# Loading the next expert's bound during the current expert's products, in the expert loop of a hybrid encoder layer

## What is computed

```
g = einsum('td,edf->tef', h, w_gate)      # w_gate: 64 x 1024 x 256
u = einsum('td,edf->tef', h, w_up)        # w_up:   64 x 1024 x 256
a = silu(g) * u * comb[..., None]         # comb is 0 but for a row's 6 experts
routed = einsum('tef,efd->td', a, w_down) # w_down: 64 x 256 x 1024
return routed + shared
```

## Time and profile before

| | us |
|---|---|
| median of 3 runs | 1249.72 |
| lowest and highest run | 1246.98, 1256.64 |
| the profiled execution, its own time | 1252.91 |
| its span, from the first instruction to the last | 1251.1 |
| TensorE busy in the span | 1103.7 |
| expert loop, first to last item's start (line 956) | 553.68 to 1152.70 |

### The profile page before, as it was taken

The page is one execution under the profiler, slowest core; times in us unless marked ns, Lnnn a source line. Parts: engine busy times, 40 slices in busy tenths (PEclk is TensorE's granted clock), DMA queues, the critical chain, the costliest instruction groups (busy, mean ns, idle before and its releaser), DMA issues.

```text
span 1251.1 us, 19602 instructions
## 1 busy us (share of the span) xinstructions
PE 1103.7 (88%) x6547; PEld 688.2 (55%) x6548; DVE 385.2 (31%) x932; ACT 338.1 (27%) x762; POOL 306.6 (25%) x500
## 2 busy tenths in 40 slices
PE   4899999898999997479999889999999989999960
PEld 1675675465675643355655455555555545555730
DVE  3100000383543224532222222222222212222687
ACT  3100100495664102212222222322323222322111
POOL 1000100102232000053333323333333323333032
PEclk9899999897987899779999999999999999999995
DMA  8711311403440003818889999998889999798652
GB/s 347 277 68 67 143 68 68 140 5 135 156 182 1 1 1 138 329 49 317 317 335 415 415 410 411 409 391 315 317 343 394 410 413 390 291 415 313 286 171 75
DMA packets 77741, 304.18 MB, mean 243 GB/s; under 512 B 13271, under 2 KB 15385, under 8 KB 59465
## 3 DMA queue, kind: packets, MB, share of 16 engines
q1 hardware_dynamic: 60792, 268.26, 54.8%
q0 software_dynamic: 16256, 33.08, 7.1%
q10 hardware_dynamic: 656, 2.36, 0.5%
HBM read 290.26 MB, written 33.82 MB: 259 GB/s over the span
## 4 chain that ended last, share of the span: by engine, by line
PE 75%; DMA 12%; DVE 7%; issue 2%; ACT 2%; POOL 1%; SPq 1%; POOLq 0%; DVEq 0%; ACTq 0%
PE bank L956 23%; PE bank L963 12%; DMA arena<-in_w_down 8%; PE bank L641 6%; PE bank L642 6%; PE bank L707 4%; PE bank L894 4%; PE bank L949 3%; DMA arena<-in_w_in 2%; PE bank L818 2%; PE bank L968 2%; DVE arena L1695 1%; PE bank L845 1%; PE bank L794 1%; PE bank L607 1%
## 5 line engine op out<-in xcount | busy, mean ns | idle before, releaser
L956 PE MATMUL bank<-arena 128*64 128x256 f32 x2880 | 336.0, 386 | 38.3 <-DMA arena<-in_w_down 17.8
L956 PEld LDWEIGHTS bank<-arena 128*64 128x64 f32 x2880 | 243.8, 139 | 163.1 <-issue 106.7
L963 PE MATMUL bank<-arena 128*64 128x512 f32 x728 | 176.3, 602 | 1.6 <-DVE arena L1652 0.8
L1658 DVE COPY arena<-bank 128x512 f32<-128x512 f32 x90 | 62.3, 692 | 365.2 <-PE bank L949 365.2
L1246 ACT COPY arena<-bank 128x128 f32<-128x128 f32 x90 | 23.9, 265 | 412.3 <-PE bank L968 412.3
L517 POOL DMA_INDIRECT arena<-h_rows,arena x93 | 98.2, 1056 | 82.7 <-POOL arena L514 78.2
L525 POOL DMA_INDIRECT y_rows<-arena x91 | 93.2, 1024 | 86.0 <-POOL arena L522 81.3
L641 PE MATMUL bank<-arena 128*128 128x288 f32 x320 | 105.5, 412 | 3.7 <-DMA arena<-in_w_in 3.7
L642 PE MATMUL bank<-arena 128*128 128x288 f32 x320 | 104.8, 410 | 0.0
L1652 DVE COPY arena<-bank 128x512 f32<-128x512 f32 x91 | 63.0, 692 | 102.1 <-PE bank L963 102.1
L963 PEld LDWEIGHTS bank<-arena 128*64 128x64 f32 x728 | 52.0, 136 | 67.4 <-issue 66.4
(11 more groups left out here) (279 smaller groups left out, 1157.2 us busy)
## 6 DMA issues: line engine op xcount, KB each, us to landing
arena<-in_w_gate SPq DMA_DIRECT2D x64, 1024.0 KB
arena<-in_w_up SPq DMA_DIRECT2D x64, 1024.0 KB
arena<-in_w_down SPq DMA_DIRECT2D x64, 1024.0 KB
arena<-in_w_ada SPq DMA_DIRECT2D x8, 2048.0 KB, 7.8
arena<-in_w_in SPq DMA_DIRECT2D x6, 2048.0 KB, 16.1
arena<-in_w_ada SPq DMA_DIRECT2D x8, 1024.0 KB, 17.3
arena<-y_rows SPq DMA_DIRECT2D x2, 3072.0 KB, 13.2
arena<-in_w_out SPq DMA_DIRECT2D x2, 2048.0 KB, 7.7
```

Of the source, the lines that this page charges most:

```text
L956: last = pe.matmul(bank[0][n * SLOT:n * SLOT + SLOT, 0:2 * P].rearrange("p (g f) -> p g f", f=P), HGT[:, k % 4, k // 4, :], w[:, :, n * P: ...
L963: last = pe.matmul(bank[3][n * SLOT:n * SLOT + SLOT, :], AE[:, f, :], DN[j][:, f, 512 * n:512 * n + 512], start=(f == 0), stop=(f == 1))
L1658: dve.tensor_copy(hgt, bank[1][:, :]).then_inc(hgt_ready, 1)
```

## The change

`item` gets an argument `ahead`. Where it is given, the engine loads `START[ahead]` between the gate and up products and the transpose of `turn_out`, and `item` returns the register. In the expert loop, `lo` and `hi` are loaded once per turn of four experts, ahead of j = 0. The first item of the experts j = 0, 1, 2 loads `START[e + j + 2]`, which is the bound of expert j + 1; after each expert the names move on: what was `hi` is now `lo`, and what was loaded is `hi`. The item of j = 3 and the items of the inner loop load nothing.

```
-            def item(i, j, before):
+            def item(i, j, before, ahead=None):
...
                 gate_up(j)
+                after = pe.value_load(START[0:1, bass.ds(ahead, 1)], min_val=1, max_val=NI) if ahead is not None else None
                 turn_out()
...
                 down(before)
+                return after
...
             with pe.Fori(0, NE // 4) as g:
                 e = g * 4
+                lo = pe.value_load(START[0:1, bass.ds(e, 1)], min_val=0, max_val=NI - 1)
+                hi = pe.value_load(START[0:1, bass.ds(e + 1, 1)], min_val=1, max_val=NI)
                 for j in range(4):
-                    lo = pe.value_load(START[0:1, bass.ds(e + j, 1)], min_val=0, max_val=NI - 1)
-                    hi = pe.value_load(START[0:1, bass.ds(e + (j + 1), 1)], min_val=1, max_val=NI)
                     pe.wait_ge(exp_ld[j], (g + 1) * 48)
                     pe.sem_inc(pe_mark)
-                    item(lo, j, (j + 3) % 4)
+                    after = item(lo, j, (j + 3) % 4, e + (j + 2) if j < 3 else None)
                     with pe.If_lt(pe.to_reg(lo + 1), pe.to_reg(hi)):
                         with pe.Fori(lo + 1, hi) as i:
                             item(i, j, j)
+                    lo, hi = hi, after
```

## The result

The changed kernel took 1245.51 us (median of 20 runs, 1238.94 to 1251.91), the kernel before, in 20 runs beside it, 1254.12 us. The ratio is 0.9937 with a 95% interval of 0.9921 to 0.9952: 7.9 us less, between 6.0 and 9.9. The forecast was 6.4 us less.

The account below looks back on a forecast made before the run. In the expert loop TensorE sets the pace in some stretches, the stream of weights in others. Of 15.5 us of gaps 6.4 are kept, 9.1 lost, the added load costs 0: 1243.3 us against the median 1249.72, range 1236 to 1250.5.

Parts of the forecast that it names:

- Part 1: At the 48 expert starts j = 1, 2, 3 no load is left; start to start becomes 6.10 us unless weights are late.
- The sum of 15.5 us: Total of 40 boundary gaps, the gain's upper bound; 8 of the 48 starts, ended by weights, are left out.
- Part 2: One load, 0.7 us, between gate-and-up and the transpose, 48 times; covered by the sequencer's lead of 2.2 us, cost 0.
- Part 3: Gaps summed by stretch of the expert loop: 6.4 us kept, 9.1 us lost where weights set the pace.
- 4.70 us: The 11 gaps from 643 to 822 us, DMA share 1.01, forecast as lost to longer waits for weights.
- halving the term: In 822 to 980 us, 4.08 us kept less half of the 2.30 behind 926, as DMAs idle little there: 2.93.
- A: Rival: TensorE is the bound throughout and all 40 gaps count; gain 15.5 us, time 1234.2, chance 0.09.
- B: Rival: weights take nearly all, also in 822 to 980 and 1025 to 1077; 2.4 us remain, time 1247.3, chance 0.13.
- C: Rival: longer waits lower TensorE's clock more often, two more places costing 3.4 us; gain 3.0, time 1246.7, chance 0.12.
- the sign that I gave for it: For the rival on the clock: more than two gate-and-up items (line 956) over 5 us.
- D: Rival: the load ahead of the transpose is not covered, 0.7 us each; +7 us, time 1256.7, chance 0.04.
- The 11 us: Issue gaps forecast to be left in the loop, from 17.0 us: those of the tops, 0.8 each.

Follow-up runs that it names:

- light_after: Changed kernel with only an eighth of the up weights loaded from the fifth expert on: 1211.90 us, ratio 0.9676 to the kernel before.
- dose6: Changed kernel with the load behind gate and up made six times instead of once: 1321.31 us, ratio 1.0594 to the kernel before.
- half: Kernel before with lo taken over from the last hi, so one load stays at the boundary, none behind gate and up: 1242.43 us, ratio 0.9929.
- rep: Changed kernel run again unaltered, for a second profile and more times: 1246.01 us, ratio 0.9956 to the kernel before.
- light: Pair with an eighth of the up weights loaded from the fifth expert on: kernel before 1232.60 us, changed kernel 1211.90 us.
- split: Pair with the down weights on a semaphore of their own, waited for ahead of the down products: kernel before 1248.98 us, changed kernel 1234.49 us.
- split_hoist: Changed kernel with a semaphore of their own for the down weights and no bound loads at the tops: 1226.98 us, ratio 0.9784.
- split_before: Kernel before with a semaphore of their own for the down weights, waited for ahead of the down products: 1248.98 us, ratio 0.9967.
- split_early: split_hoist with the wait for the down weights moved ahead of the wait for the evacuated transpose: 1218.89 us, ratio 0.9723 to the kernel before.

## Why the prediction was right, point by point

**Part 1, the loads that go: right.** Starts in time are at 6.10, VectorE's product is late next and leaves no gap. The sum of 15.5 us is near what light_after shows: 18.9 in the loop, where the 8 starts that the sum left out count too. Of these 8, 7 are ended by weights. The eighth (1028.04) is late because the item ahead of it is the slow one at 1019.91; the profile shows 0.20 us of issue there and no wait for weights, so its gap belonged into the sum (some 0.3 to 0.4 us).

**Part 2, the load that comes in costs 0: right.** The lead fell from 2.26 to 1.49 us, where 1.5 was forecast, and dose6 shows what it covers. But the argument missed that the boundary itself has room for one load (half): the cover was not needed. The Trainium skill, "DMA: Bandwidth & Descriptors", section "Latency and other measured facts", has a floor of about 600 ns for a tensor load; the rows have 0.31 us for the instruction, which is under that floor, and 0.65 to 0.77 with its arithmetic, and the measurement decides. As forecast, nothing hung on it.

**Part 3, the split into kept and lost: right in its pattern, three terms off.** I compare the loops by the starts of the same items: of before and after in the profiles shown, and of the second profile (rep). Starts in the kernel before, then in the changed kernel, of the first item of experts 0, 8, 29, 44, 55 and 62 (numbered from 0):

```profile
553.68 6.29 PE L956 MATMUL bank<-arena 128*64 128x256 f32 x32 [1.73 <-DVE arena L1645]
...
646.03 3.67 PE L956 MATMUL bank<-arena 128*64 128x256 f32 x32 [0.78 <-issue]
...
822.27 3.67 PE L956 MATMUL bank<-arena 128*64 128x256 f32 x32 [2.24 <-DMA arena<-in_w_down]
...
983.12 3.67 PE L956 MATMUL bank<-arena 128*64 128x256 f32 x32 [0.76 <-issue]
...
1085.76 3.67 PE L956 MATMUL bank<-arena 128*64 128x256 f32 x32 [0.16 <-issue]
...
1140.21 3.67 PE L956 MATMUL bank<-arena 128*64 128x256 f32 x32 [1.89 <-DMA arena<-in_w_down]
```

```profile
554.18 6.25 PE L956 MATMUL bank<-arena 128*64 128x256 f32 x32 [1.74 <-issue]
...
644.28 3.67 PE L956 MATMUL bank<-arena 128*64 128x256 f32 x32 [0.78 <-issue]
...
980.32 3.67 PE L956 MATMUL bank<-arena 128*64 128x256 f32 x32 [0.79 <-issue]
...
1082.96 3.65 PE L956 MATMUL bank<-arena 128*64 128x256 f32 x32
...
1138.02 3.67 PE L956 MATMUL bank<-arena 128*64 128x256 f32 x32 [1.70 <-DMA arena<-in_w_down]
```

(Expert 29 starts at 821.16 in the changed kernel, in a row above.)

| from expert to expert | forecast | after | rep |
|---|---|---|---|
| 0 to 8 | -2.2 | -2.3 | -2.3 |
| 8 to 29, paced by weights | 0 | +0.6 | +0.4 |
| 29 to 44 | -2.9 | -1.7 | -4.0 |
| 44 to 55 | -1.1 | 0.0 | -1.1 |
| 55 to 62, paced by weights | 0 | +0.6 | +0.5 |
| 62 to the last | -0.3 | -0.3 | -0.3 |
| loop | -6.4 | -3.0 | -6.7 |

Between 8 and 29 the stretch did not get shorter, as forecast: all of its 4.70 us are lost, and a little of what was gained ahead of it. From 29 to 44 rep kept 4.0 of the 4.08 us, so halving the term was wrong: the DMAs could give that much. In the first profile the open slow item at 821.16 took 1.7 of it. half has that slow item too, at 823.20, and its stretch is 2.6 us shorter, so the halved 2.9 lies among what the three profiles show, but not for the reason given. The last stretch paced by weights also took back about 0.5 us. The pattern was right, and that the total came out near is in part luck: the errors offset each other, and 6.4 came out for a measured 7.9 (6.0 to 9.9).

**The rivals.** A (all gaps count) is refuted for this kernel by the waits that grew to 28.9 us, and is what happens once weights are no bound: 20.7 us in light, 14.5 in split. B (the weights take nearly all) fell with the stretch from 29 to 44. C (the clock falls more often) happened beside the forecast: 4 and 3 items over 5 us against 2, so the sign that I gave for it was met in both profiles. Its price was not: two stood open in the first profile, but only the one at 821.16 cost its 1.7 us, and in rep none did. What I said against it, that the next item waits for its weights anyway, did not hold for the kernel before itself: the item behind the slow one at 1019.91 shows no such wait, in the row below. I had given C as the other case; it belonged into the forecast's own spread.

```profile
1028.04 3.67 PE L956 MATMUL bank<-arena 128*64 128x256 f32 x32 [0.20 <-issue]
```

D (the load not covered) is refuted by the lead, and its price is seen in dose6.

The check "issue gaps fall to about 11, waits for weights grow to about 27" met 9.0 and 28.9 in the first profile, without the gap ahead of the loop. The 11 us counted the tops at 0.8 each; 4 of the 15 tops are ended by weights now, where it was 2.

## What to carry to other kernels

A gap that closes is worth its length only as far as the next place where transfers set the pace: sum gaps by stretch, with the DMA share beside them, and count a full stretch as nothing. Look which of several loads behind one wait lands last and when it is used; here a semaphore of its own for the down weights made the same edit worth nearly twice as much. A register load by the engine's sequencer is hidden where the sequencer has lead over the array or waits for something later anyway, and the second of two is the one that shows.

## What the runs showed of the hardware

- A load of a register with its check took 0.77 us of the sequencer's lead for the first in a row and 0.65 for each further one, of which `TENSOR_LOAD` itself is 0.30 to 0.31 us; single ones took up to 0.89 us.
- In the kernel before, TensorE's sequencer ran 2.26 us ahead of the array by the end of the 32 gate and up matmuls, the same at nearly all items.
- A semaphore wait (with the mark behind it) that no row shows as waiting for weights still left a gap of about 0.19 us per item (16.7 in 90) and took 0.15 to 0.17 us from start to start (6.25 in split_hoist and 6.27 in split_before against 6.10) when it stood behind the latest wait, and nothing ahead of it (6.10 in split_early).
- The same wait for weights (3.47 and 3.52 us at one item) was followed by an item of 5.36 us at a granted clock of 0.68 in one execution, and of 3.67 us at 1.00 in another. The clock also fell after gaps of 2.18 us (dose6) and 1.97 us (670.87).
- An item at the lower clock cost its 1.7 us where TensorE set the pace behind it (821.16), and nothing in the end where the weights did (670.87).
